# A two-block model on one core: all 52 input tiles as three products of rounded halves and rests

## The reference, cut to what matters

```
u = rmsnorm(x, norm1_w)
proj = u @ w_in                      # 1024 -> 6672 columns: q, f_pre, i, g, z, x, B, C, dt
hgrn2 (8 heads of 128): f = lb + (1-lb)*sigmoid(f_pre); k = 1-f; log_f = log(f)
        cumulated log_f gives the decays; scores, state and output of each head, then a norm and a gate
mamba2 (16 heads of 64): causal conv on x, B, C; dt = softplus(dt_pre + bias); scan; gated norm
x = x + concat(hgrn2, mamba2) @ w_out;  then a gated feed-forward with a short conv
second block: modulation, retention, 16 experts of which each takes 32 tokens
```

## Time and profile before

| | us |
|---|---|
| median of 3 runs | 1702.42 (1701.29 to 1703.94) |
| the profiled execution | 1704.49 |
| its span, first to last instruction | 1702.7 |
| PE busy / ACT busy / DVE busy in the span | 1349.4 / 450.4 / 507.1 |
| TensorE's mean granted clock | 0.896 of full speed |

### The profile page before, as it was taken

One profiled execution on the slowest core, in us unless ns is written; L12 is line 12 of the kernel. 1 busy time (PEld: TensorE's weight loads), 2 busy tenths in 40 slices (PEclk: granted clock), 3 DMA queues, 4 the chain that ended last, 5 costly groups with the idle time before them and its releaser, 6 DMA issues.

```text
span 1702.7 us, 21054 instructions
## 1 busy us (share of the span) xinstructions
PE 1349.4 (79%) x8581; PEld 831.1 (49%) x8581; DVE 507.1 (30%) x919; ACT 450.4 (26%) x675; POOL 232.8 (14%) x100
## 2 busy tenths in 40 slices
PE   6989999999999999988767577666657667666665
PEld 4877788879998988944222122112212221221221
DVE  3874677436568455622000000000000000000001
ACT  4853465436564533721000000000000000000001
POOL 0000000028767654400000000000000000000000
PEclk9999999999999999997887878888887877987887
DMA  7936322168534552285999999999999999999995
GB/s 242 361 149 235 112 99 100 50 210 273 186 137 181 201 188 99 100 357 212 428 429 428 429 428 429 428 428 429 429 429 428 429 429 428 429 428 429 428 428 250
DMA packets 92335, 524.01 MB, mean 308 GB/s; under 512 B 8009, under 2 KB 30945, under 8 KB 64369
## 3 DMA queue, kind: packets, MB, share of 16 engines
q1 hardware_dynamic: 92057, 523.08, 75.4%
q10 hardware_dynamic: 216, 0.06, 0.0%
HBM read 522.08 MB, written 1.05 MB: 307 GB/s over the span
## 4 chain that ended last, share of the span: by engine, by line
DMA 47%; PE 38%; DVE 8%; ACT 3%; issue 1%; SPq 1%; POOL 0%; ACTq 0%; DVEq 0%
DMA ring<-in_w_down 23%; DMA ring<-in_w_up 23%; PE ps L657 6%; PE ps L661 6%; PE ps L658 6%; PE ps L1213 3%; PE ps L890 3%; PE ps L1226 3%; PE ps L872 2%; PE ps L1123 2%; PE ps L641 1%; SPq L502 1%; DVE arena L2024 1%; PE ps L802 1%; PE ps L706 1%
## 5 line engine op out<-in xcount | busy, mean ns | idle before, releaser
L1213 PE MATMUL ps<-ring,arena 128*32 128x512 f32 x1984 | 297.5, 745 | 163.2 <-DMA ring<-in_w_up 136.0
L1599 POOL TENSOR_TENSOR ring_r<-ring,ring_r 128x1024 fp32r<-128x1024 f32 (+1 forms) x96 | 232.6, 2441 | 483.3 <-ACT ring_r L1265 483.3
L657 PE MATMUL ps<-arena_r,ring_r 128*128 128x258 f32 (+3 forms) x960 | 289.3, 301 | 9.7 <-PE ps L661 3.4
L661 PE MATMUL ps<-arena_r,ring_r 128*128 128x258 f32 (+3 forms) x960 | 281.4, 293 | 0.0
L1226 PE MATMUL ps<-ring,arena 128*32 128x512 f32 x1024 | 171.2, 804 | 104.1 <-DMA ring<-in_w_down 97.1
L1213 PEld LDWEIGHTS ps<-ring,arena 128*32 128x32 f32 x1984 | 65.0, 127 | 378.3 <-DMA ring<-in_w_up 204.7
L657 PEld LDWEIGHTS ps<-arena_r,ring_r 128*128 128x128 f32 x960 | 183.2, 191 | 20.6 <-issue 13.2
L661 PEld LDWEIGHTS ps<-arena_r,ring_r 128*128 128x128 f32 x960 | 182.4, 190 | 2.9
L658 PE MATMUL ps<-arena_r,ring_r 128*128 128x256 f32 (+2 forms) x608 | 180.8, 297 | 0.0
L2239 DVE TENSOR_TENSOR arena<-arena,ps 128x512 f32<-128x512 f32 x16 | 11.0, 688 | 448.7 <-PE ps L1213 448.7
L1226 PEld LDWEIGHTS ps<-ring,arena 128*32 128x32 f32 x1024 | 33.0, 129 | 225.1 <-DMA ring<-in_w_down 147.6
(11 more groups left out here) (370 smaller groups left out, 1478.1 us busy)
## 6 DMA issues: line engine op xcount, KB each, us to landing
ring<-in_w_gate SPq DMA_DIRECT2D x64, 2048.0 KB, 25.9
ring<-in_w_down SPq DMA_DIRECT2D x64, 2048.0 KB, 26.2
ring<-in_w_up SPq DMA_DIRECT2D x60, 2048.0 KB, 21.9
ring<-in_w_in SPq DMA_DIRECT2D x20, 2048.0 KB, 11.7
ring<-in_w_ada SPq DMA_DIRECT2D x12, 2048.0 KB, 8.5
ring<-in_ffn_w_up SPq DMA_DIRECT2D x22, 1024.0 KB, 7.9
ring<-in_w_out SPq DMA_DIRECT2D x6, 2048.0 KB, 8.0
ring<-in_ffn_w_down SPq DMA_DIRECT2D x4, 2048.0 KB, 8.4
```

Source lines behind the costliest of these rows:

```text
L657: pe.matmul(o, hi[:, k, :], r_(xhi(k0 + k)), start=first and k == 0, stop=False)
L661: mm = pe.matmul(o, lo[:, k, :], r_(xhi(k0 + k)), start=False, stop=last and k == nk - 1)
L1213: mm = pe.matmul(ps[32 * j:32 * j + 32, half, :], xs[:, kt, :], wk[:, 512 * j:512 * j + 512], start=kt == 0, stop=kt == KT - 1)
L1599: pool.tensor_tensor(r_(w), w, f_(rounded(c)), ALU.subtract).then_inc(ev("w_lo"), 1)
```

## The change

All 52 tiles are split, and the dt columns too. The first norm is made on tokens: ScalarE squares the tokens row by row and takes roots, VectorE divides, TensorE turns the raw and the normed tokens (24 transposes each), ScalarE writes the rounded half of `uT` on the way out of PSUM and VectorE the rest. Only the identity (64 KB) is loaded ahead of the tokens, the other constants behind the first weights; the first weights wait for nothing, and seven small loads move from ScalarE's queue to SyncE's, behind the first weights. In the heads, f isn't written any more (Ln takes scale and bias), `hg_cumulate` goes two heads ahead, in the third tile of a round, `hg_decay` moves into the first tile, and `hg_log` and `hg_log_mean` into the third.

```diff
-SPLIT = range(2, 28)
+SPLIT = range(NPROJ)
 ...
-            load(cst[:], a["cst"], "cst_loaded")
+            load(cst[:, 0:P], a["cst"][:, 0:P], "ident_loaded")
 ...
-                if u == 0:
-                    sp.wait_ge(ev("par_loaded"), 16 * PAR_LOADS[0])
 ...
+                if u == 0:
+                    rows("lb0", r1(a["hg_lb_logits"][0:1]))
 ...
+                    load(cst[:, P:NCST], a["cst"][:, P:NCST], "cst_loaded")
 ...
-                    done(group([(wsm[:, 0, k, :], uT[:, k, :]) for k in range(KT)], o[0:16, 0:T]))
+                    pe.wait_ge(ev("dt_split"), 2)
+                    done(group([(r_(w[:, k, :]), r_(x[:, k, :])) for k in range(KT)
+                                for w, x in ((dt_hi, uT), (dt_hi, uT_lo), (dt_lo, uT))], o[0:16, 0:T]))
 ...
             def hg_log(h):
-                act.wait_ge(ev("hg_f"), h + 1)
-                act.activation(hg_lf, hg_f, ACT.Ln).then_inc(ev("hg_log"), 1)
+                if h:
+                    act.wait_ge(ev("hg_b"), h)
+                else:
+                    act.wait_ge(ev("m2_out"), 8)
+                lb, oml = small[:, 96 + h:97 + h], small[:, 104 + h:105 + h]
+                act.activation(hg_lf, proj[:, h + TF_, :], ACT.Ln, scale=oml, bias=lb).then_inc(ev("hg_log"), 1)
 ...
                 if (j - 32) % 3 == 0:
                     hg_keys(h)
-                    if h:
-                        hg_log_mean(h - 1)
-                    if h + 1 < HEADS:
-                        hg_log(h + 1)
+                    if j + 3 < NPROJ:
+                        round_weights(f"i{j + 3}")
+                    if h == 0:
+                        hg_log(1)
+                    elif h + 1 < HEADS:
+                        hg_exps(h + 1)
                     if h:
                         hg_inverse(h - 1)
                     act.wait_ge(ev("hg_out"), h + 1)
                     if h:
                         act.wait_ge(ev("hg_mean"), h)
                     act.activation(hg_sq, ps[:, 6, 0:T], ACT.Square).then_inc(ev("hg_squared"), 1)
-                    if h + 1 < HEADS:
-                        hg_exps(h + 1)
-                if (j - 32) % 3 == 2 and h == HEADS - 1:
+                    if h == 0:
+                        hg_exps(1)
+                if (j - 32) % 3 == 2:
                     hg_log_mean(h)
-                    hg_inverse(h)
+                    if h + 2 < HEADS:
+                        hg_log(h + 2)
 ...
-                if j + 3 in SPLIT:
+                if j + 3 < NPROJ and (j < 32 or (j - 32) % 3):
                     round_weights(f"i{j + 3}")
 ...
                     hg_states(h)
+                    if j + 3 < NPROJ:
+                        in_rest(j + 3)
                     if h == 0:
                         mod_add(1)
-                    if h + 1 < HEADS:
-                        hg_cumulate(h + 1)
+                    if h == 0:
+                        hg_cumulate(1)
+                    elif h + 1 < HEADS:
+                        hg_decay(h + 1)
                 if (j - 32) % 3 == 1:
                     hg_gate(h)
                     if h:
                         hg_finish(h - 1)
-                    if h + 1 < HEADS:
-                        hg_decay(h + 1)
+                    else:
+                        hg_decay(1)
+                if (j - 32) % 3 == 2 and h + 2 < HEADS:
+                    hg_cumulate(h + 2)
 ...
-                if j + 3 in SPLIT and j + 3 > SPLIT[1]:
+                if j + 3 < NPROJ and (j < 32 or (j - 32) % 3):
                     in_rest(j + 3)
```

More of the change, by code:

```diff
@@ L239, in build @@
         chan = A.take(2, T)[0:16]
-        xin_lo = Arena(WORDS - 8 * T - 16).take(4, T)
-        def uin(part, k):
-            if part == 0:
-                return proj[:, (TF_, TQ)[k // 4] + 4 + k % 4, :]
-            return proj[:, TI + 4 + k, :] if k < 4 else xin_lo[:, k - 4, :]
+        m2_halves = A.take(1, T)[0:48, 0]
+        m2_pick = A.take(1, 16)[0:48, 0]
+        dt_hi = A.take(KT, 16)
+        dt_lo = A.take(KT, 16)
+        uT_lo = Arena(WORDS - KT * T).take(KT, T)
+        at = A.at
+        normed = Arena(0).take(3, D)
+        norm1 = Arena(at + 3 * P).take(8)
+        sums1, root1, inv1 = (Arena(at + 3 * P + 8 + 4 * i).take(4) for i in range(3))
+        squares1 = Arena(3 * D).take(D)
         A = Arena(x_at)
@@ L258, in build @@
         hg_inv = A.take(1, T)[:, 0]
-        hg_f, hg_k, hg_lf, hg_sq = (proj[:, TBM + i, :] for i in range(4))
+        hg_k, hg_lf, hg_sq = (proj[:, TBM + i, :] for i in range(1, 4))
         A = Arena(x_at)
@@ L479, in rounded @@
             return ring[:, RING - 1, at:at + nk * P].rearrange("p (k c) -> p k c", k=nk)
-        seq = [f"x{k}" for k in range(KT)] + ["n1"]
+        seq = [f"x{k}" for k in range(5, KT)] + [f"y{k}" for k in range(KT)]
         for j in range(NPROJ):
@@ new lines, in _ @@
+            act.wait_ge(ev("tok_loaded"), 64)
+            for w in range(3):
+                n = WINDOWS[w][1]
+                st.link(act.activation(squares1[0:n], tok[0:n, w, :], ACT.Square, accum_out=sums1[0:n, w:w + 1]))
+                act.activation(root1[0:n, w:w + 1], sums1[0:n, w:w + 1], ACT.Sqrt, scale=1.0 / D, bias=eps[0:n, 0:1]).then_inc(ev("root1"), 1)
+            for k in (5, 6, 7):
+                act.wait_ge(ev("tiles_done"), TN[f"x{k}"] + 1)
+                act.activation(hT[:, k, :], bank_of(f"x{k}")[:, 0:T], ACT.Copy).then_inc(ev("tiles_freed"), 1)
@@ new lines, in _ @@
+            for k in range(5):
+                act.wait_ge(ev("x_turned"), k + 1)
+                st(act.activation(hT[:, k, :], ps[:, 3 + k, 0:T], ACT.Copy))
+            st.wait()
+            act.wait_ge(ev("tiles_freed"), 3)
+            act.nop().then_inc(ev("stream_tiles"), KT)
+            act.wait_ge(ev("start_steps"), 3)
+            for k in range(KT):
+                act.wait_ge(ev("tiles_done"), TN[f"y{k}"] + 1)
+                act.activation(r_(uT[:, k, :]), bank_of(f"y{k}")[:, 0:T], ACT.Copy, scale=norm1[:, k:k + 1]).then_inc(ev("u_hi"), 1)
+                if k == 2:
+                    round_weights("i0")
@@ L1638, in _ @@
             st.link(tt(lb, small[:, 0:8], small[:, 24:32], ALU.mult))
+            noml = small[:, 112:120]
+            st(ts(noml, lb, -1.0, None, ALU.add))
             st.link(ts(oml, lb, -1.0, 1.0, ALU.mult, ALU.add))
@@ L1905, in _ @@
                 if j == 4:
[L1907 removed]
+                    dve.wait_ge(ev("par_turned"), 3)
                     for b in (1, 2, 3):
```

157 lines of the change are left out of this document (85 added, 72 removed).

## The result

The changed kernel takes 1725.11 us (median of 4 runs, 1724.27 to 1727.08) where the kernel before, beside it, takes 1702.99: a ratio of 1.0134, 95% interval 1.0118 to 1.0151. It is slower, as forecast, but by 22 us in place of 8, above the top of the range (1716). The profiled execution took 1724.92 us, its span is 1723.1, 20.4 more than before's 1702.7; I account for these 20.4.

What follows compares the result with a forecast made beforehand. TensorE was taken to bound up to tile 27, and in the heads a VectorE and ScalarE loop as long as TensorE's work. Terms -5.0 - 0.8 + 8.15 + 2.4 - 3.3 + 6.6, together +8.0 on 1702.4, gave 1710.4 us, range 1697 to 1716.

Steps and rivals of the forecast that it cites:

- start: Ahead of tile 4: weights issued without SyncE's 7.8 us wait, less 2.8 for more issues; -5.0 us, bounds 0 and -7.8.
- dt: The dt columns: 16 products of 3.83 us become 24 of 3.0, all on the path; -0.8 us.
- to head 1's values: Head 0's round: a rounding and rests queue ahead of gate and decay, so head 1's values come 8.15 us later.
- five rounds without the clock: Head 1's to head 6's values: a chain through three engines takes 85.1 us against 82.73; +2.4 us.
- behind head 6's values, without the clock: From head 6's values to head 7's output: tiles 50 and 51 start earlier and are shorter, scans already done; -3.3 us.
- the clock: TensorE's waits in the heads bring half-speed stretches behind them; +6.6 us, bounds 0 and 9.9.
- I take the sum: At the start: full -5.0 us taken, assuming 24 more transposes are offset by work dropped ahead of tile 0.
- 17.3 + 16.0 + 17.3 + 17.3 + 17.2: Predicted lengths in us of rounds 1 to 5, sum 85.1; ScalarE's path sets most, VectorE binds round 2.
- C: Rival, chance 0.17: VectorE alone sets the heads' rounds at 16.05 us, so -3.2 in all, 1699.2 us.
- with two in three: In the heads: two of three TensorE waits bring half clock, so 1.1 us for each of six stretches, +6.6.
- B: Rival, chance 0.2: the heads' waits bring no half clock or it falls on slack; +1.4, 1703.8 us.
- D: Rival, chance 0.08: TensorE binds all along, rounds of 14.0 us and no delay in head 0; 1677 us.

Runs made afterwards that it cites:

- e1_fill: The changed kernel with TensorE making the level products of the scores twice in heads 1 to 7, ahead of its wait for the values; 1720.05 us.
- e3_logs_first: e2_rests_behind with the mean's Ln and the log ahead of the third tile's rounding on ScalarE; 1709.08 us.
- e2_rests_behind: The changed kernel with VectorE's rests in the heads moved: the second tile's behind gate, finish and decay, the third's behind the next head's decay; 1717.58 us.
- e5_fill_more: e1_fill with a third set of the level products for heads 2, 5 and 6; 1716.78 us.
- e7_early_log: e2_rests_behind with ScalarE's log right behind the square and the mean's Ln in the next round behind the keys; 1714.53 us.
- f2_old_order_split: The changed kernel with k, scans, differences, logs, exps and decays in the order of before, all tiles split, rests and roundings left in place; 1741.74 us.
- f3: f2_old_order_split with VectorE's three rests moved to where it waits for the exps, and ScalarE's first rounding behind the logs; 1705.14 us.
- f1: The changed kernel with tiles 32 to 51 plain and the heads in the order of before, f still not written; 1700.49 us.

## Why the prediction was right and wrong

Each term, as forecast and as measured. The columns add up to the 8.0 that was predicted and the 20.4 between the two spans.

| term | forecast | measured | from |
|---|---|---|---|
| start | -5.0 | -3.47 | tile 4 at 39.98 against 43.45 |
| dt | -0.8 | -0.36 | the `ada` behind it at 84.17 against 88.00, 3.8 in all |
| to head 1's values | +8.15 | +9.45 | 213.37 - 207.75 + 3.8 |
| five rounds without the clock | +2.4 | +7.1 | 89.83 - 82.73 |
| behind head 6's values, without the clock | -3.3 | -2.52 | 17.67 - 20.44, and 0.25 behind head 7's |
| the clock | +6.6 | +10.2 | 7.9 and 2.3 |

**The start.** The mechanism was right and one bound of it was named. The weights landed five microseconds earlier, as forecast, but then they weren't the last to come. Tile 4's rest was done at 38.2; TensorE, which began tile 0 at 23.02 where before began it at 26.54 and then worked almost without a break, came to tile 4 at 39.98. The bound had this case ("TensorE, with 24 more transposes"); "I take the sum" was 1.5 too much. The 1.5 have a place: the first 17 of tile 0's 24 products stand some 0.225 us apart, the later ones 0.125, though the clock column reads 1.00 there. Tile 0 took 4.9 us in place of 3.1; at 3.1 TensorE would have been at tile 4 by 38.2, just with the rest. In e1_fill and e3_logs_first tile 0 starts at the same 22.83, 22 and 16 products are slow, and the first `ada` comes at 38.88 and 37.77.

```profile
24.32 0.43 PE L668 MATMUL ps<-uT_r,ring_r 128*128 128x272 f32 x1
24.55 0.43 PE L664 MATMUL ps<-uT_r,ring_r 128*128 128x272 f32 x1
...
28.75 0.29 PE L664 MATMUL ps<-uT_r,ring_r 128*128 128x272 f32 x1
28.87 0.29 PE L665 MATMUL ps<-arena_r,ring_r 128*128 128x272 f32 x1
```

Of dt's row, dt itself gave 0.60 (the `ada` ahead of it is 3.23 earlier than before, the one behind it 3.83); 0.24 was lost between tile 4 and there.

**Head 0.** The step "ScalarE does these exps before it evicts tile 32 and rounds tile 36, and VectorE's rest of tile 36 stands ahead of the gate" came out to the letter: VectorE stood 5.58 us, TensorE 6.70. The 1.3 us that are missing stand ahead of the heads already: TensorE's clock was 0.69 over 162.5 to 168.0, in tiles 28 and 29, and took back what these two save. That is read from the trace, and it isn't the whole account: e1_fill, with the same lists up to there, had 1.00 in that stretch and stood at head 0's values 1.5 us sooner behind dt's `ada` (100.56 us against 102.07), but lost 1.2 of it in head 0's round, where the clock over the 5 us behind the 3.56 us wait was 0.50 in place of 0.71. What a clean clock ahead of the heads would be worth at head 1 stays open. e2_rests_behind and e3_logs_first shortened this round from 27.1 to 24.9 and 23.8 us.

**The rounds.** The failed step is the size of "17.3 + 16.0 + 17.3 + 17.3 + 17.2". It was 18.6, 17.2, 17.9, 17.9 and 18.3 without the clock. Two reasons were shown by e5_fill_more's rows: the sum of ScalarE's own durations from square to log left out what the list waits for, tile B's end (round 2: "there VectorE binds" was wrong by 1.2) and the finish behind a rest (0.6 in a silu round, 1.8 in round 5). The third is round 1's late square, 0.7, of which some may be the experiment's own. That ScalarE's list and not VectorE's sum makes the round, the ground on which C had 0.17, was shown by e2_rests_behind, e3_logs_first and the clean rounds, of which e2's own two took the forecast's 17.3; C's own rounds of 16 to 17 were then reached by moving one rounding.

**The clock.** The failed step is "with two in three". All six waits were paid, and two of the stretches were longer than the 3.3 us of the earlier trace rows: the one from head 6's values ran at a mean of 0.57 over 6.2 us. All six paid in full were to cost 9.9; measured were 10.2. The Trainium skill (TensorE: Matmul & The Clock Gate, Part 1) says that the half rate is the default and that activity releases it. The trace of the changed kernel agrees with it; that each of these waits would be long enough was the prediction's own step, and the page doesn't say it. The discount came from a wait of 2.0 us, and the waits to be judged were of 2.2 to 3.8. But a rule of "every wait" wouldn't have been right either: 2.08 us left the clock at 1.00 in e3_logs_first and 2.12 brought it to 0.66, and e7_early_log has 2.77 us followed by 0.67 and 2.78 by 1.00.

**Behind head 6.** -3.3 was right within the small waits, and the clock took most of it back.

**The rivals.** B (no clock) fell with e1_fill, C with e2_rests_behind, and D's 14 us a round was never seen. The chances under "How the numbers follow" don't add up as said: B's 0.2 and half of C's 0.17 are 0.285 already, more than the 0.25 given to "within", so "slower" had 0.55 at most. The sum of my errors is 12.4 us: 2.0 at the start and dt, 1.3 at head 0, 4.7 in the chain, 0.8 behind it, 3.6 in the clock. They had one direction. A chain's sum built from durations alone is a lower bound, each link of it can wait for a fourth thing, and the range's top of 1716 allowed for one such wait only.

## What to carry to other kernels

Where an order is spread over in-order engines, ask of each new operation what it waits for and what stands behind it, before its duration: a rest of 1.2 us cost 5.6 us in front of a gate, in one round in the changed kernel and in each in f2_old_order_split, and splitting the heads' tiles cost 41 us with the rests in the wrong places, 4.7 with them where VectorE was idle (f2 and f3 against f1). When two changes come together, run the square: the new order was a loss by itself and a gain with the split, and neither could be read from the pair. And to know what a half clock costs, let TensorE repeat products during its waits whose repetition leaves the result as it is: the difference is the clock's price, less what the repeats themselves hold up.

## What was not expected of the hardware

VectorE's operations on two SBUF operands stood still while GpSimd ran a subtraction of 128x1024 beside them: 5.49 us for 2.57, 3.41 for 1.43, 3.38 for 1.29. Idle GpSimd is no free helper to a chain on VectorE.

Waits of TensorE between 1.9 and 2.8 us fell on either side, and their length doesn't decide. Ahead of L820 the clock stayed at 1.00 behind 1.94 and 2.78 us (e7_early_log), 2.08, 2.09, 2.11 and 2.42 (e3_logs_first), 2.55 and 2.71 (e2_rests_behind); half rate followed 1.96 (e1_fill), 2.10 (e2), 2.12 (e3), 2.16 and 2.55 (the changed kernel) and 2.77 (e7). In the heads of these kernels single waits of 1.4 to 1.5 us were not followed by it, and every one of 3.18 us or more was.
